# Modulation of both layers: eight units ahead of the first projection, forty in the first attention, in four column strips

## What is computed

```python
for l in range(DEPTH):                                   # DEPTH = 2
    mod_lat = (silu(c) @ w_mod[l] + b_mod[l])            # w_mod[l]: 1024 x 6144
    mod_ctx = (silu(c_ctx) @ w_mod[l] + b_mod[l])
    sh1, sc1, g1, sh2, sc2, g2 = split(mod_lat, 6)       # the same for the context
    h = rms_norm(x, norm_pre_mix[l]) * (1.0 + sc1) + sh1
    y = mixer(h)            # l = 0: GQA attention and HGRN2; l = 1: neighbourhood attention
    x = x + g1 * rms_norm(y, norm_post_mix[l])
    h = rms_norm(x, norm_pre_ffn[l]) * (1.0 + sc2) + sh2
    x = x + g2 * rms_norm(conv_ffn(h), norm_post_ffn[l])
```

## Time and profile before

| what | value |
|---|---|
| median of 3 runs | 4055.62 us (4049.09 to 4056.63) |
| the profiled execution, its time | 4051.7 us |
| its span, first to last instruction | 4049.9 us |
| mean granted clock of TensorE | 0.96 |
| instructions | 72020 |
| TensorE busy | 92% of the span |
| VectorE, ScalarE busy | 19%, 18% |
| moved by DMA | 635.40 MB |

### The profile page before, as it was taken

How to read it: one execution, slowest core, us unless ns; L and a number is a source line. 1 busy time by engine, 2 the same in 40 slices (tenths; PEclk the granted TensorE clock), 3 DMA queues, 4 the chain that set the end, 5 groups by cost and what they waited for, 6 DMA issues and landing times.

```text
span 4049.9 us, 72020 instructions
## 1 busy us (share of the span) xinstructions
PE 3726.5 (92%) x30842; PEld 2842.5 (70%) x30843; DVE 783.6 (19%) x1600; ACT 711.7 (18%) x1436; POOL 116.3 (3%) x153
## 2 busy tenths in 40 slices
PE   7999966899998999999899999897999999999988
PEld 3455454344444667878678888687898889988888
DVE  0121494311102042211321011322000000101001
ACT  1213331222102133211111011111111111100001
POOL 0000000100001001001000001000000000000000
PEclk9999988999999999999899999898999999999999
DMA  8214300122122213334134344133898889864457
GB/s 307 97 66 151 129 1 21 52 73 73 61 84 73 78 42 116 137 121 153 65 106 145 141 143 151 63 117 149 338 348 336 313 313 368 331 228 151 141 207 286
DMA packets 93485, 635.40 MB, mean 157 GB/s; under 512 B 10384, under 2 KB 11408, under 8 KB 37136
## 3 DMA queue, kind: packets, MB, share of 16 engines
q1 hardware_dynamic: 91904, 627.78, 41.9%
q0 software_dynamic: 1424, 5.24, 0.4%
HBM read 631.93 MB, written 1.05 MB: 156 GB/s over the span
## 4 chain that ended last, share of the span: by engine, by line
PE 88%; DVE 7%; issue 2%; ACT 2%; DMA 1%; POOL 0%; SPq 0%; ACTq 0%; DVEq 0%; POOLq 0%
PE bank L362 28%; PE bank L638 18%; PE bank L408 16%; PE bank L428 4%; PE bank L336 4%; PE bank L372 4%; PE bank L595 2%; PE bank L443 2%; PE bank L466 2%; PE bank L326 1%; PE bank L653 1%; PE bank L456 1%; DVE SC L1286 1%; DVE RT L1126 1%; DVE Y L1143 1%
## 5 line engine op out<-in xcount | busy, mean ns | idle before, releaser
L362 PE MATMUL bank<-H,ring 128*128 128x256 f32 (+1 forms) x3744 | 1074.7, 450 | 23.9 <-ACT H L799 20.9
L362 PEld LDWEIGHTS bank<-H,ring 128*128 128x128 f32 x3744 | 716.4, 192 | 378.3 <-issue 305.9
L408 PE MATMUL bank<-PROJ,ring 128*64 128x96 f32 (+2 forms) x7776 | 667.9, 282 | 16.7 <-ACT SC L833 8.7
L408 PEld LDWEIGHTS bank<-PROJ,ring 128*64 128x64 f32 (+1 forms) x7776 | 547.6, 147 | 136.5 <-issue 104.1
L638 PE MATMUL bank<-MIX,ring 128*64 128x96 f32 x12544 | 539.9, 251 | 30.0 <-issue 29.8
L638 PEld LDWEIGHTS bank<-MIX,ring 128*64 128x64 f32 x12544 | 536.2, 140 | 34.4 <-issue 34.3
L336 PE MATMUL bank<-ring,cs 128*2 128x256 f32 x768 | 174.9, 381 | 27.3 <-DMA ring<-in_mod 22.1
L1454 DVE TENSOR_TENSOR PROJ<-SC,bank 128x96 f32 (+2 forms) x246 | 70.9, 288 | 663.7 <-ACT SC L979 659.6
L638 PE MATMUL bank<-H,ring 128*128 128x256 f32 x896 | 195.7, 382 | 0.0
L638 PEld LDWEIGHTS bank<-H,ring 128*128 128x128 f32 x896 | 171.7, 192 | 24.3 <-issue 0.6
L428 PE MATMUL bank<-H,ring 128*128 128x256 f32 x768 | 174.3, 384 | 0.0
(11 more groups left out here) (271 smaller groups left out, 2449.8 us busy)
## 6 DMA issues: line engine op xcount, KB each, us to landing
ring<-in_moe_up SPq DMA_DIRECT2D x224, 1024.0 KB, 5.4
ring<-in_moe_down SPq DMA_DIRECT2D x128, 896.0 KB, 5.9
ring<-in_mod SPq DMA_DIRECT2D x48, 1024.0 KB, 4.8
ring<-in_up SPq DMA_DIRECT2D x44, 1024.0 KB, 4.8
ring<-in_tproj SPq DMA_DIRECT2D x32, 1024.0 KB, 4.8
ring<-in_proj SPq DMA_DIRECT2D x26, 1024.0 KB, 4.8
ring<-in_gates SPq DMA_DIRECT2D x24, 1024.0 KB, 4.8
ring<-in_down SPq DMA_DIRECT2D x32, 704.0 KB, 4.0
```

The costliest lines, as they stand in the source:

```text
L362: mm = pe.matmul(B[(tile + t) % 4][:, 0:width], w[:, k, t * P:(t + 1) * P], src[:, k, 0:width], start=k == 0, stop=k == k_n - 1)
L408: mm = pe.matmul(B[bank][lo:lo + m, 0:width], w[:, k, lo:lo + m], src(s * half + k), start=s == 0 and k == 0, stop=s == 1 and k == half - 1)
```

## The change

- `mod0` and `mod1` become `mod_a`, 8 units (the sh1 and sc1 of layer 0) ahead of the projection, and `mod_b`, the other 40 units (the rest of layer 0 and all of layer 1), in the first attention. `mods_at` spreads them over its 32 iterations: one in each, and a second one in every fourth, behind the value products. In the attention they share one bank, as before.
- A unit runs in four column strips. `cs` is now 128 x 32 for each of the eight inputs, with 30 columns of zeros, and lies in MIX; product k goes to the strip of partitions 32 (k mod 4) to 32 (k mod 4) + 31, so each strip sums two of the eight products. `mod_row` copies all 128 partitions, and `mod_turn` is a product with the 128 x 2 matrix `sel`, which sums the four strips while it turns.
- The loads change order. A small first load `fst` brings the condition vectors and `sel` (18 columns); then come four units of the ring, X, the other four, the constants, the parameters, and the projection's units.
- TensorE's first wait is for `fst`; it waits for constants and parameters after the eight units. On ACT the squares of X come between the fourth and the fifth row copy. On DVE only the factor for the first norm is made ahead of it; the other three factors of layer 0 follow the attention.

```diff
+MOD_A = 8
-    STAGES += [("mod0", 24, SLOT), ("proj0", 14, SLOT), ("mod1", 24, SLOT)] if _l == 0 else [("proj1", 12, SLOT)]
+    STAGES += [("mod_a", MOD_A, SLOT), ("proj0", 14, SLOT), ("mod_b", 48 - MOD_A, SLOT)] if _l == 0 else [("proj1", 12, SLOT)]
...
-        cs = sb("cs", [P, KT, 2])
+        fst = sb("fst", [P, FIRST["_end"]])
+        cs = MIX[:, 6, 0:32 * KT].rearrange("p (k c) -> p k c", c=32)
...
+        MROW = MIX[:, 7, :].rearrange("p (s t) -> p s t", s=2)
+        def mod_bank(n):
+            return B[4 + 2 * (n % 2) if n < MOD_A else 4][:, 0:2 * P]
+        def mods_at(i):
+            n = 48 - MOD_A
+            return range(MOD_A + n * i // 32, MOD_A + n * (i + 1) // 32) if i < 32 else ()
...
-            sp.dma_start(cst[:, :], dram["consts"]).then_inc(S("consts_in"), 16)
-            sp.dma_start(par[:, :], dram["params"]).then_inc(S("params_in"), 16)
-            sp.dma_start(flat(X[:, :, :]), dram["xT"]).then_inc(S("x_in"), 16)
+            sp.dma_start(fst[:, :], dram["first"]).then_inc(S("first_in"), 16)
...
                     for u in range(NSLOT):
                         sp.dma_start(ring[:, u, 0:w], src[u]).then_inc(slot_full[u], 16)
+                    sp.dma_start(flat(X[:, :, :]), dram["xT"]).then_inc(S("x_in"), 16)
                     stream(name, NSLOT, n - NSLOT, src[NSLOT:n])
+                    sp.dma_start(cst[:, :], dram["consts"]).then_inc(S("consts_in"), 16)
+                    sp.dma_start(par[:, :], dram["params"]).then_inc(S("params_in"), 16)
...
+            def mod_unit(n):
+                w = unit(mod_u(n)).rearrange("p (k n) -> p k n", n=2 * P)
+                if n >= 2:
+                    pe.wait_ge(S("mod_row"), n - 1 if n < MOD_A else n)
                 for k in range(KT):
-                    mm = pe.matmul(B[mod_bank(l, j)][0:2, 0:2 * P], cs[:, k, :], w[:, k, :], start=k == 0, stop=k == KT - 1)
+                    lo = 32 * (k % 4)
+                    mm = pe.matmul(mod_bank(n)[lo:lo + 32, :], cs[:, k, :], w[:, k, :], start=k < 4, stop=k >= 4)
                 mm.then_inc(unit_done, 1)
...
+            def mod_turn(n):
+                pe.wait_ge(S("mod_row"), n + 1)
                 for t in range(2):
-                    mm = pe.transpose(B[5][:, 4 * j + 2 * t:4 * j + 2 * t + 2], rows[0:2, j % 2, t * P:(t + 1) * P], ident[0:2, 0:2])
+                    mm = pe.matmul(B[5][:, 4 * n + 2 * t:4 * n + 2 * t + 2], MROW[:, n % 2, t * P:(t + 1) * P],
+                                   fst[:, FIRST["sel"]:FIRST["sel"] + 2], start=True, stop=True)
                 mm.then_inc(S("mod_t"), 1)
...
+            def mod_step(n):
+                mod_unit(n)
+                if n > MOD_A:
+                    mod_turn(n - 1)
...
                     if l == 0:
-                        mod_step(1, i)
+                        for m in mods_at(i)[:1]:
+                            mod_step(m)
+                        if i == 32:
+                            mod_turn(47)
                     if 2 <= i < n + 2:
                         turn(us[i - 2])
...
                     if i >= 3:
                         values(us[i - 3])
+                    if l == 0:
+                        for m in mods_at(i)[1:]:
+                            mod_step(m)
...
+            pe.wait_ge(S("first_in"), 16)
+            pe.wait_ge(S("cs_ready"), 2)
+            for m in range(MOD_A):
+                mod_unit(m)
+                if m > 0:
+                    mod_turn(m - 1)
+            mod_turn(MOD_A - 1)
             pe.wait_ge(S("consts_in"), 16)
             pe.wait_ge(S("params_in"), 16)
-            pe.wait_ge(S("cs_ready"), 1)
-            for i in range(25):
-                mod_step(0, i)
             norm(0, TC)
...
+            def mod_row(n):
+                act.wait_ge(unit_done, mod_u(n) + 1)
+                if n >= 2:
+                    act.wait_ge(S("mod_t"), n - 1)
+                act.activation(MROW[:, n % 2, :], mod_bank(n), ACT.Copy).then_inc(S("mod_row"), 1)
...
-                    if l == 0 and i < 24:
-                        mod_row(1, i)
+                    if l == 0:
+                        for m in mods_at(i):
+                            mod_row(m)
                         hgrn_early(i)
...
+            for m in range(MOD_A // 2):
+                mod_row(m)
+            squares(0, X, TC, S("x_in"), 16, 0)
+            for m in range(MOD_A // 2, MOD_A):
+                mod_row(m)
             act.wait_ge(S("params_in"), 16)
             act.wait_ge(S("consts_in"), 16)
...
-            mod_vectors(0)
-            mod_factors(0)
+            mod_vectors(0, MOD_A)
+            mod_factors(0, 0, 1)
             modulate(0, 0, TC)
             gqa_prep()
             attention(0)
-            mod_vectors(1)
+            mod_vectors(MOD_A, 48)
+            mod_factors(0, 1, 4)
             hgrn(0)
```

More of the change, by code:

```diff
@@ L51 @@
                   ("rcount", 4 * T), ("ones_row", T), ("iota", CAP), ("eps", 1)])
-PARAMS = columns([("c", KT * 2)] + [(f"b_mod{l}", 48) for l in range(DEPTH)]
+FIRST = columns([("c", KT * 2), ("sel", 2)])
+PARAMS = columns([(f"b_mod{l}", 48) for l in range(DEPTH)]
                  + [(f"n{i}_{l}", KT) for l in range(DEPTH) for i in range(4)]
@@ L152, in build @@
         tile_base, tb = {}, 0
-        ntiles = {"mod0": 0, "mod1": 0, "proj0": 22 + 12, "proj1": 16 + 16, "moe_up": N_EXPERTS * 2 * ET, "moe_down": N_EXPERTS * KT}
+        ntiles = {"mod_a": 0, "mod_b": 0, "proj0": 22 + 12, "proj1": 16 + 16, "moe_up": N_EXPERTS * 2 * ET, "moe_down": N_EXPERTS * KT}
         for l in range(DEPTH):
@@ L205, in build, with mod_u @@
         att_of = [[u for u in range(len(ATT)) if ATT[u][0] == l] for l in range(4)]
-        def mod_bank(l, j):
-            return 4 + 2 * (j % 2) if l == 0 else 4
+        MROW = MIX[:, 7, :].rearrange("p (s t) -> p s t", s=2)
+        def mod_bank(n):
+            return B[4 + 2 * (n % 2) if n < MOD_A else 4][:, 0:2 * P]
+        def mod_u(n):
+            return base["mod_a"] + n if n < MOD_A else base["mod_b"] + n - MOD_A
+        def mods_at(i):
+            n = 48 - MOD_A
+            return range(MOD_A + n * i // 32, MOD_A + n * (i + 1) // 32) if i < 32 else ()
         def gates_at(i):
@@ L289, in _ @@
                 src = dram[name]
-                if name == "mod0":
+                if name == "mod_a":
                     for u in range(NSLOT):
                         sp.dma_start(ring[:, u, 0:w], src[u]).then_inc(slot_full[u], 16)
+                    sp.dma_start(flat(X[:, :, :]), dram["xT"]).then_inc(S("x_in"), 16)
                     stream(name, NSLOT, n - NSLOT, src[NSLOT:n])
+                    sp.dma_start(cst[:, :], dram["consts"]).then_inc(S("consts_in"), 16)
+                    sp.dma_start(par[:, :], dram["params"]).then_inc(S("params_in"), 16)
                 elif name == "moe_up":
@@ L986, in swiglu @@
                     pair(j, 0)
+            act.wait_ge(S("first_in"), 16)
+            act.wait_ge(S("cs_ready"), 1)
+            act.activation(cs[:, :, 0:2], fst[:, 0:2 * KT].rearrange("p (k s) -> p k s", s=2), ACT.Silu).then_inc(S("cs_ready"), 1)
+            act.sem_inc(lin_free, 4)
+            for m in range(MOD_A // 2):
[3 more added lines that the diff above has]
+                mod_row(m)
             act.wait_ge(S("params_in"), 16)
             act.wait_ge(S("consts_in"), 16)
[L990 to L994, removed]
             root(0, TC)
@@ L1150, in plain_norm, with mod_vectors, mod_factors @@
                                              op0=ALU.mult, op1=ALU.mult).then_inc(sem, 1)
[L1152 to L1160, removed]
+            def mod_vectors(n0, n1):
+                dve.wait_ge(S("mod_t"), n1)
+                bm = W("b_mod0", 96)[:, 2 * n0:2 * n1]
+                dst = MOD[:, :, :, :].rearrange("p l a b -> p (l a) b")[:, 2 * n0:2 * n1, :]
+                dve.tensor_tensor(dst, B[5][:, 4 * n0:4 * n1].rearrange("p (a b) -> p a b", b=2),
+                                  bm.unsqueeze(2).to_broadcast([P, 2 * (n1 - n0), 2]), ALU.add).then_inc(S("mod_ready"), 1)
+            FACTORS = ((8, True), (16, False), (32, True), (40, False))
+            def mod_factors(l, i0, i1):
+                dve.wait_ge(S("mod_ready"), 1 if i1 == 1 else 2)
                 if l > 0:
                     dve.wait_ge(S("norm3_out"), KT)
-                for i, (row, pre) in enumerate(((8, True), (16, False), (32, True), (40, False))):
+                for i in range(i0, i1):
+                    row, pre = FACTORS[i]
                     w = W(f"n{i}_{l}", KT).unsqueeze(2).to_broadcast([P, KT, 2])
@@ L1491, in router @@
                                   ALU.mult).then_inc(S("rt_wr"), 1)
+            dve.memset(cs[:, :, :], 0.0).then_inc(S("cs_ready"), 1)
+            dve.wait_ge(S("masks_in"), 16)
+            step(dve.tensor_copy(lmask[:, :], SC[:, :]))
             dve.wait_ge(S("consts_in"), 16)
             dve.wait_ge(S("params_in"), 16)
-            dve.wait_ge(S("masks_in"), 16)
```

(15 more changed lines are left out.)

12 lines of the change are left out of this document (removed).

## The result

The changed kernel takes **3896.6 us** (median of four runs, 3894.4 to 3898.0) against 4054.8 for the kernel before: a ratio of 0.961, interval 0.960 to 0.963. That is 158 us less where 96.7 were forecast, and outside the range (3943 to 3985). Three places have to be read apart: the start, the attention, and the experts, which no line of the change touches. Between the two profiled executions (spans 4049.9 and 3896.2) the differences in time to the first projection, to HGRN's first matmul and to the experts' first are -70.2, -74.6 and -72.8 us; the experts and what follows them add another 81.

What follows compares the result with a forecast made beforehand. TensorE was taken as the bound (88% of the chain), behind a transfer queue at the start. Start -72.9, attention -24.4 and DVE +0.6 sum to -96.7 us, forecasting 3959 us against the median 4055.6; range 3943 to 3985.

Steps and rivals of the forecast that it cites:

- start: Up to the first projection: transfers end at about 39.2 us, then the norm; projection at 54.1 instead of 127.0, -72.9 us.
- unit / its products, full clock: First attention: a modulation unit in four strips takes 0.97 us, the two products replacing its transposes 0.43 us.
- four iterations: First attention: four iterations with five units, their products and 0.8 us of waits take 16.5 us; 134.1 us after scaling.
- ScalarE's early work: First attention: sigmoid, table loads and passes for HGRN, less covered by shorter units, add 4 us (0 to 7).
- clock in the attention: First attention: a pause of 3 us at ScalarE's work may put the clock down once, +2 us (0 to 4).
- attention in all: First attention with 40 units instead of 24: 140.1 us against 164.5, -24.4 us.
- from the attention to the experts: Between attention and HGRN: three small DVE operations for layer 0's other factors leave the norm's shadow, +0.6 us.
- The 2 us for a norm out of idleness: Start: 2 us added to the norm because TensorE stands idle before it and its clock is low (0 to 7).
- neither two nor three: Attention rivals: two strips at once, unit 1.85 us, 3993 us, chance 0.13; three strips' worth, 1.26 us, 3970 us, 0.13.
- The ring: Attention rival: unit transfers become the bound below 286 GB/s; at 250 GB/s +19 us, 3978 us; chance 0.05.
- The ends of its own range: 3943: unit 0.89, no clock loss, ScalarE's work hidden; 3969: norm wholly at 1.2 GHz, 7 us of ScalarE.
- the rival of two strips: Attention: array takes only two streams at once, unit 1.85 us, +34 us, 3993 us; chance 0.13.

Runs made afterwards that it cites:

- ScalarE's passes moved: Changed kernel with ScalarE's four early HGRN passes moved out of the first attention into the three token units ahead of it; 3873.4 us (0.956).
- the run with the pauses filled: Changed kernel with seven and six unread matmuls in TensorE's two long waits and 204 semaphore increments at TensorE's start; 3892.4 us.
- a good place: Kernel before with 126 semaphore increments ahead of TensorE's first wait, no part of the change in it; 3967.2 us (0.980).
- the strips alone with ScalarE's passes moved: Changed kernel with 24 units ahead and 24 in the attention, ScalarE's four early HGRN passes moved out of it; 3889.5, 3892.1, 3918.0 and 3940.1 us.

## Why the prediction was wrong

| term | predicted | measured |
|---|---|---|
| start | -72.9 (projection at 54.1) | -70.2 (56.85) |
| unit / its products, full clock | 0.97 / 0.43 us | 1.00 / 0.47 |
| four iterations | 16.5 us | 17.07 |
| ScalarE's early work | +4 (0 to 7) | +5.8 |
| clock in the attention | +2 (0 to 4) | +15.7 |
| attention in all | -24.4 | -4.8 |
| from the attention to the experts | +0.6 | +1.8 |
| the experts | no term | -81 |

- **The start was right.** The norm came 1.3 us later than the transfers' sum said. The 2 us for a norm out of idleness were there (9.19 against 7.13), and a table load of 1.28 us that the norm used to cover stands in the open at 49.81. The transfers ran at 420 GB/s from 20 to 40 us. At the 358 GB/s of the Trainium skill ("DMA: Bandwidth & Descriptors", Specifications) they would, by an estimate, have taken 6.6 us longer than the forecast had it, not 1.3. The trace lies above that figure, which the page gives as a stack's bandwidth divided by two cores; here one core runs.
- **The strips were right.** Four at once, neither two nor three: the starts come in fours, the sign that the prediction named. That is 3.5 times (3.54 / 1.00), more than the 2.38 and 3.07 that the Trainium skill ("TensorE: Matmul & The Clock Gate", Part 3) has for three column and four row strips. The waits for a row copy came where they were put: 0.30, 0.30 and 0.49 us in four iterations. The ring was no bound: with ScalarE's passes moved the attention took 138.0 us at 313 GB/s.
- **The step that failed in the attention** is "a pause of 3 us there may put the clock down once: +2 (0 to 4)". The passes were seen, the pauses were seen, and their length was about right. What was mis-sized is what follows a pause: one fall with a loss of 2 us is some 4 us at half clock, and there were two, of 13.7 and 27.3. TensorE sets the pace there, so most of the low clock is paid (half of 41.0 us would be 20.5), and the run with the pauses filled shows its 15.7 us by themselves. The attention came out 19.4 us over the forecast (159.5 against 140.1): 13.7 of these are the clock, 1.8 the passes, and 3.9 the iterations (138.0 without passes and falls, against 134.1).
- **The step that is missing altogether** is the experts. The sum has no term for them: it puts the rest of the kernel at no change, without a reason. No instruction of theirs changes, but 192 were added ahead of them, and that moved their loop. They measured -81 us, which is what put the time outside the range. The trace of the kernel before had the signs: stalls of 4.01 and 2.95 us with no releaser at the second expert, 133 packets in the instruction queue where the changed kernel has 70. The prediction's own have one too: 34.3 us in which the weight loads of the experts' line stood with no releaser; after the change it is 11.2. The prediction drew nothing from them. That a loop that touches eight blocks is refetched and one of seven is not fits all runs (nine packets per expert would be eight and the next one). The trace does not show the blocks' boundaries, so the count itself is argued; that the place and the length decide, by some 82 us, is shown both ways.
- **The signs of failure all lay in the two places that the change touches**: a unit over 1.5 us, a projection after 60, a wait for the ring. None of them came (1.00, 56.85, no wait), and the forecast failed all the same. The ends of its own range also do not follow from the terms named with them: these give some 3948 and 3967, not 3943 and 3969. The outcome does not turn on that.

With the loop in the place where it stood before, the changed kernel takes 3979.9 us. That is inside the range and 21 over the forecast, of which the clock's 15.7 - 2 is the most. So without the experts the time would have lain inside the range although the step on the clock was wrong, and that by luck: the upper bound had been raised for the rival of two strips, which did not come. So the change as it was understood is worth 71 us with the loop in a good place (3967.2 to 3896.6) and 72 in the bad one (4052.0 to 3979.9); the other 82 or so are a matter of placement, which the kernel before could have had without it.

## What to carry to other kernels

When a hot loop's code is a few of the instruction queue's packets long, look at that queue: if packets recur in every iteration, move the loop's start (here 126 semaphore increments at the program's start did it) before anything else is tuned, and compare two kernels only with the loop in the same place. After making TensorE's work in an interleaved stage cheaper, list what its longer instructions used to cover on the other engines: here passes that were free under 3.54 us units became two pauses, and the half clock behind the pauses cost 15.7 us where the passes themselves cost 5.8. A wait names the last engine in a chain; follow it to the one that was really late.

## What the runs showed of the hardware

- A loop of 1631 TensorE instructions either runs from the second iteration on without one fetch or fetches nine packets of 16.4 KB in each, with 7 to 8 us of stalls at its turn and some 10 us or more of half clock behind them, by a shift of 64 instructions.
- In the strips alone with ScalarE's passes moved, a pause of 2.16 us was followed by 112.6 us at half clock, with TensorE busy for 111.8 of them. In the three other executions of that kernel, which were not profiled, the time was 22 to 51 us shorter. In the changed kernel pauses of 3.35 and 2.74 us were followed by 13.7 and 27.3 us.
- A semaphore increment on TensorE takes 0.16 us: 192 of them lasted until 30.4 us, 204 until 32.3.
